# Transposes of the identity put into TensorE's queue at the front of three stages of an encoder layer

## The reference, cut to what matters

```
h = rms_norm(x) * (1 + scale(c)) + shift(c)
q, k, v, gate | c_q, c_kv, k_rope, gate = split(h @ w_in)
stick-breaking heads: z = q k / 8;  w = exp(log_sigmoid(z) + sum over later keys of log_sigmoid(-z));  w v
latent heads:         softmax over keys up to the query's block of 64;  p v
y = x + gate(c) * rms_norm(concat(both * silu(gates)) @ w_out)
```

## Time and profile before

| | us |
|---|---|
| runs of the kernel before, median (lowest to highest) | 2458.39 (2457.03 to 2458.82) |
| the profiled execution, its time | 2456.41 |
| its span, first to last instruction | 2454.6 |
| PE busy, matmuls (x12100) | 2193.4, 89% |
| PE weight loads | 1833.6, 75% |
| DVE / ACT / POOL busy | 1346.5 / 1326.9 / 897.8 |
| granted PE clock, mean of the span | 0.951 of full |
| where the stages begin, by the first instruction after the barrier | columns 401.7, attention 1019.3, last stage 2045.4 |

### The profile page before, as it was taken

The page is one execution under the profiler, slowest core; times in us unless marked ns, Lnnn a source line. Parts: engine busy times, 40 slices in busy tenths (PEclk is TensorE's granted clock), DMA queues, the critical chain, the costliest instruction groups (busy, mean ns, idle before and its releaser), DMA issues. The chain is left out here.

```text
span 2454.6 us, 39802 instructions
## 1 busy us (share of the span) xinstructions
PE 2193.4 (89%) x12100; PEld 1833.6 (75%) x12100; DVE 1346.5 (55%) x2773; ACT 1326.9 (54%) x2868; POOL 897.8 (37%) x931
## 2 busy tenths in 40 slices
PE   5999996999988899589999999999999992999998
PEld 1888885999987577457777777777777781787886
DVE  3232224100138333277878777878787872767773
ACT  3233223121123333268888888888888883467553
POOL 0000000000000000164848484848484834646673
PEclk9999997999989999779999999999999995999999
DMA  7433333222347799744343433333333114676772
GB/s 277 138 94 101 104 110 101 91 71 92 112 154 198 247 315 320 224 84 92 73 90 70 90 70 88 71 89 70 89 71 89 42 31 144 184 224 190 207 226 86
DMA packets 295696, 320.16 MB, mean 130 GB/s; under 512 B 88929, under 2 KB 219004, under 8 KB 290578
## 3 DMA queue, kind: packets, MB, share of 16 engines
q1 hardware_dynamic: 290034, 299.90, 43.5%
q10 hardware_dynamic: 3456, 11.14, 1.2%
q0 software_dynamic: 2048, 7.41, 0.8%
HBM read 199.09 MB, written 110.90 MB: 126 GB/s over the span
## 5 line engine op out<-in xcount | busy, mean ns | idle before, releaser
L1350 ACT ACTIVATE pa_whi<-banks 128x512 fp32r<-128x512 f32 (+3 forms) x640 | 345.5, 540 | 98.9 <-PE banks L1576 80.1
L1576 PE MATMUL banks<-ident,pa_p 128*128 128x128 f32 x2176 | 354.5, 279 | 2.2 <-ACT pa_p L1315 2.2
L1559 PE MATMUL banks<-pa_khi,pa_qst 128*128 128x512 f32 (+3 forms) x640 | 260.8, 407 | 102.1 <-DVE pa_p L1411 76.0
L1504 POOL TENSOR_TENSOR pa_wlo<-pa_whole,pa_whi 128x512 fp32r<-128x512 f32 (+2 forms) x240 | 277.6, 1171 | 140.8 <-ACT pa_whole L1355 140.4
L1576 PEld LDWEIGHTS banks<-ident,pa_p 128*128 128x128 f32 x2176 | 267.8, 143 | 61.6 <-issue 5.1
L1536 PE MATMUL banks<-pa_whi,pa_vst 128*128 128x512 f32 (+3 forms) x640 | 285.7, 447 | 4.1 <-POOL pa_wlo L1504 3.0
L1411 DVE TENSOR_TENSOR_SCAN pa_p<-banks,pa_p,pa_zero 128x512 f32<-128x512 f32 x192 | 246.4, 1283 | 70.9 <-ACT banks L1308 65.4
L1559 PEld LDWEIGHTS banks<-pa_khi,pa_qst 128*128 128x128 f32 x640 | 125.3, 196 | 177.5 <-DVE pa_p L1411 136.7
L1388 DVE TENSOR_TENSOR pa_wlo<-banks,pa_whi 128x512 fp32r<-128x512 f32 (+3 forms) x400 | 234.9, 587 | 33.3 <-ACT pa_whi L1350 31.2
L1560 PE MATMUL banks<-pa_klo,pa_qst 128*128 128x512 f32 (+3 forms) x640 | 242.7, 379 | 0.0
L662 POOL DMA_DIRECT2D gate_ada<-in_ada_w_dram x2 | 1.8, 898 | 646.2 <-DVE qu_wlo L718 646.2
(11 more groups left out here) (262 smaller groups left out, 5291.2 us busy)
## 6 DMA issues: line engine op xcount, KB each, us to landing
scratch_sb_kT<-ke_kT SPq DMA_DIRECT2D x12, 1024.0 KB, 9.0
scratch_mla_kT<-ke_nT SPq DMA_DIRECT2D x12, 1024.0 KB, 5.7
scratch_mla_v<-ke_v SPq DMA_DIRECT2D x12, 1024.0 KB, 5.3
scratch_gatesT<-co_gates SPq DMA_DIRECT2D x12, 704.0 KB, 11.3
ada<-in_ada_w_dram SPq DMA_DIRECT2D x4, 2048.0 KB, 10.6
pr_x<-in_x_prompt_dram SPq DMA_DIRECT2D x16, 512.0 KB, 4.0
scratch_hT<-pr_hT SPq DMA_DIRECT2D x16, 512.0 KB, 5.0
ke_k<-in_cache_sb_k_dram SPq DMA_DIRECT2D x8, 1024.0 KB, 7.8
```

The source lines that it names most:

```text
L1350: act.activation(whi[:, t % NW, q0:], bank, ACT.Copy).then_inc(hi_done, 1)
L1504: pool.tensor_tensor(wlo[:, t % NW, q0:], whole[:, t % 4, q0:], raw(whi[:, t % NW, q0:]), ALU.subtract).then_inc(pool_lo, 1)
L1559: pe.matmul(bank, qst[job][:, q], khi[job][:, keys], start=True, stop=False)
L1576: y = pe.transpose(ps[:, NS + t % NTB, x * P:(x + 1) * P], probs[g][x][:, i * P:(i + 1) * P], s["ident"][:])
```

## The change

A helper that transposes the identity into a given bank n times is called at five places of PE's queue: 80 times before the first tile of columns, into bank 7; 160 times in the attention, behind the two waits quoted above and before the first chunk, into bank 6; in the last stage 50 times before the first slot and 12 times in each of the slots from -11 to -5, behind the slot's score, into bank 7. `pe.transpose(bank, ident, ident)` is one weight load and one matmul of 128 x 128, f32.

```diff
+def keep_going(pe, bank, ident, n):
+
+    for _ in range(n):
+        pe.transpose(bank, ident, ident)
@@ columns_phase, PE
+                keep_going(pe, ps[:, 7, 0:P], s["ident"][:], 80)
                 turns(pe, lambda p, b, _: None, back, peeled=1)
@@ prompt_attention_phase, PE
+                keep_going(pe, ps[:, 6, 0:P], s["ident"][:], 160)
                 for m in range(LEAD):
                     chunk(0, m)
                 steps_in_turn(pe, step)
@@ tail_phase, PE
+                keep_going(pe, ps[:, OUT + 2, 0:P], s["ident"][:], 50)
                 for t in slots:
                     if 0 <= t + AHEAD < U:
                         score(t + AHEAD)
+                    if t < -EARLY:
+                        keep_going(pe, ps[:, OUT + 2, 0:P], s["ident"][:], 12)
                     if 0 <= t < U:
                         turn(t)
```

## The result

With the change the kernel takes **2466.32 us**, the median of 11 runs (2461.05 to 2469.42), against 2458.82 before, also of 11 (2454.23 to 2461.84). The ratio is 1.0032, 95% interval 1.0023 to 1.0041: slower by 7.5 us. The forecast was 2465.6 us.

What follows compares the result with a forecast made beforehand. PE was taken as busy nearly everywhere, its clock low in few slices, among them the three stages' fronts. Columns 0, attention +7.7 and last stage -0.5 gave +7.2 on a median of 2458.39: 2465.6 us, range 2456 to 2474.

Steps and rivals of the forecast that it cites:

- A: Forecast: transposes raise the clock but outlast the attention's wait by 8.7 us; most clock lost before use; 2465.6 us; chance 0.66.
- One transpose and the clock's rise: All three fronts: 0.21 us per transpose cold, 0.116 warm; full clock after 5 us, ends 3.4 and 6.
- What comes back in the attention: Attention's first chunks: clock kept for two rounds, -1.0 us against the 8.7 late; term +7.7.
- Columns, 0: Columns' front: 80 transposes delay nothing; clock low again at 423.1, same 5 us of half speed; term 0.
- The estimate of 2.6 for a clock that is held: Columns' dense work: if the clock were kept, 16 matmuls at 0.29 instead of 0.16, plus eighth triple; -2.6 us.
- Last stage, -0.5: Last stage: fourth score on the chain warm, 0.8 less, 0.5 kept; clock fallen by 2088.4; ends -4.6 and +3.
- The price given for that end, -4.6: Last stage's dense work at full clock: 2.5 us from 12.6 matmuls and 1.6 at the second fall.
- The sum: Whole kernel: columns 0, attention +7.7, last stage -0.5, together +7.2 us.
- B: Rival: transposes do not raise the clock; attention +21.5, about +27 in all, 2485 us; chance 0.12.
- C: Rival: attention's front keeps the clock to its end, worth -4.4; +3.8 in all, 2462.2 us; chance 0.14.
- D: Rival: clock kept in all three fronts (-2.6, -4.4, -4.6), attention's overrun 5.0; -6.6, 2451.8 us; chance 0.08.

Runs made afterwards that it cites:

- e8: Only the columns' 80 transposes, plus 8 after each of the first seven triples, against the kernel before: 2457.33 us, ratio 1.0001.
- e1: Only the attention's 160 transposes, against the kernel before: 2463.83 us, ratio 1.0025.
- e4: Only the attention's transposes, 90 instead of 160, against the kernel before: 2456.92 us, ratio 0.9997.
- e6: Only the attention's transposes, 320 instead of 160, behind the two waits, against the kernel before: 2482.75 us, ratio 1.0103.
- e7: Only the attention: 90 transposes in front and 4 after each of the twenty first chunks, against the kernel before: 2454.94 us, ratio 0.9992.
- e10: e7 and e8 together, nothing added in the last stage, against the kernel before: 2454.25 us, ratio 0.9984.
- e11: e7 and e8 together with the last stage of e9, against the kernel before: 2452.83 us, ratio 0.9980.
- e12: The whole change with 90 transposes in the attention instead of 160, against the kernel before: 2456.86 us, ratio 0.9997.
- e2: Only the columns' 80 transposes, against the kernel before: 2459.55 us, ratio 1.0008.
- e3: Only the last stage's 50 and 7 x 12 transposes, against the kernel before: 2458.51 us, ratio 1.0001.
- e9: Only the last stage: no 50 or dozens, but 85 and 36 transposes just ahead of its dense work, against the kernel before: 2460.16 us, ratio 1.0006.

## Why the prediction was right, point by point

**Which case came.** A, the forecast, and the step that carried it: the attention's transposes outlast the wait. It measures 7.3 us late where 8.7 stood. Their start was 1030.88, not 1027.3: they stood behind ScalarE's `pa_hide`, as foreseen, but that came 3.6 us later because the load of its constant landed later (9.2 us after its issue, 6.1 in the trace of before). The loads of this front are all later in this execution, the keys by 3.1, so the end they race against moved along. The transposes are not the reason: in e8, which has none in this stage, the first chunk stands 22.9 us after the stage's first instruction, before 20.1. What remains: transposes that took 18.9 us instead of 20.8 (-1.9), and a start 0.5 later against the keys; -1.4.

**One transpose and the clock's rise.** 0.116 warm was too high, 0.107 measured, and 0.21 cold was 0.20. The rise came after 3.0 to 3.9 us, below the 5 taken, once below its low end of 3.4. These two terms are what made 18.9 of the 20.8. The short rise is luck of this execution: in front of the same chunks it came after 4.8 to 5.9 us in seven other kernels (e1, e4, e6, e7, e10, e11, e12).

**What comes back in the attention.** Two warm rounds, -1.0: the first chunks take 27.6 us instead of 28.6, and the clock goes 4.6 us after the first of them. Term: 7.3 - 1.0 = +6.3 where +7.7 stood; e1's runs say +5.4.

**Columns, 0.** The clock rose at 405.9, was held for five triples and was low again at 419.5, behind a wait of 2.48 us; the dense work started cold. e2's +1.1 lies within its interval. The estimate of 2.6 for a clock that is held came out at 2.3 in e8, e10 and e11.

**Last stage, -0.5.** The first half went as told: 62 transposes took 8.9 us (9.4 foreseen). What failed is small: by luck of the last dozen the clock was up at 2100.6 in the changed kernel (and for 0.8 us at 2089.37 in e3), which the text had among its ends and not as what it took. It bought nothing there, as the second dense stretch was at half clock for some 6 us instead of 3.4. The price given for that end, -4.6, did not arrive: it counted every matmul's saving as the stage's. In e9, warm throughout, the first stretch's 2.5 us came to 1.8 at the wait for GpSimd's low part and to 0.8 behind it, and the second stretch's 1.6 came whole, but none of it was left at the end. The term measured is 0 (e3 +0.1, e9 +2.3, neither clear of no difference), not -0.5.

**The sum.** 0 + 7.7 - 0.5 = 7.2 against 7.5 measured. By the parts' own runs it is 1.1 + 5.4 + 0.1 = 6.6; the difference is within what the intervals allow. That the sum came within 0.3 us is better than its terms were, and so in part luck: the attention's was some 1.4 to 2.3 too high, the last stage's 0.5 too low.

**The rivals.** B is out: with transposes alone on PE, the rows at 405.90, 1034.00 and 2061.40 show 1.00. The Trainium skill, page "TensorE: Matmul & The Clock Gate", section "Part 4: PE-mode transpose", says that the full clock doesn't engage for them; for transposes of this form (float32, identity by identity) every trace here says otherwise. C and D are out for this change, as the clock fell in the first chunks and in the columns. But e7, e8 and e10 show that the prices behind them were fair for the stretch itself: 3.5 us where 4.4 stood, 2.3 for 2.6. D's -4.6 for the last stage was too high, and neither it nor the attention's 3.5 has to reach the end of its stage.

## What to carry to other kernels

Filler work on an engine with one queue in order is free only as long as it ends before the wait does, and every instruction beyond that is paid in full at the end of the stage: size it by the end of the wait in the trace, with a margin for loads that land some 3 us earlier or later, and put it ahead of other waits that the real work has anyway. Raising the clock in front of sparse work buys a few us of it; to gain, the filler has to go on between the sparse pieces, within waits that PE has there. Ask who is late next: where GpSimd's low part was, 1.0 of the 1.8 us saved on PE only lengthened the wait. And when the gain is some 3 us, follow it by one instruction from stretch to stretch, since falls of the clock in untouched code can move the end of a stage by as much.

## What the runs showed that was not expected

Transposes of the identity into an unused bank raise the granted clock from 1.2 to 2.4 GHz by themselves, after 2.7 to 6.1 us where PE had been idle before, and kept it up for 16 us (149 of them, 0.107 us each) and for some 32 us in e6 (296 of them). The soonest and the latest rise are both in the columns: e2, whose transposes start at 401.7, has full clock from 404.5 at the latest, and e12, whose start at 402.1, is at half clock until 408.1 at least:

```profile
404.50:411.90 7.40, 7.40 (x70) 7.40 (x69) 6.71 (x4) 6.76 (x5) 0.00 (x0) 1.00 0.38 112
```
```profile
402.20:408.10 5.90, 5.90 (x28) 5.90 (x29) 3.65 (x2) 5.85 (x4) 0.00 (x0) 0.50 0.24 80
```

Very little was needed to hold it: 4 of them per chunk kept it over 23 us in which PE was busy for 17.5 (e7), where 14.2 of 22.9 without them ran at half clock.

The attention differs by some 3 us from one profiled execution to the next in kernels that add nothing to it, as much as the best of these edits gains. Two things make it up in the traces. One is when the first keys land: in e8, whose attention is 3.2 us longer than before, 2.8 of them are there at the first chunk. The other is short stretches of half clock further on, as in the rows at 1178.20 and 1068.70 above, which come in some executions and not in others and cost up to some 1 us each there, and more near the end of the last stage. What makes the clock fall in them was not tested.
